# Fetching compression pages over two queues: two pages of each group of four by GpSimd, two by SyncE

## The reference

```python
old = pool[page_table].reshape(B, -1, N_KV_HEADS, HEAD_DIM)
...
def compress(rows, pe, w1, b1, w2):
    B, L, KV, DH = rows.shape
    n_chunk = L // STRIDE_CMP
    c = rows[:, :n_chunk * STRIDE_CMP].reshape(B, n_chunk, STRIDE_CMP, KV, DH)
    w1r = w1.reshape(BLOCK_CMP, DH, CMP_HID)
    lead = jnp.einsum('bnlkd,ldf->bnkf', c + pe[:STRIDE_CMP, None, :], w1r[:STRIDE_CMP])
    trail = jnp.einsum('bnlkd,ldf->bnkf', c + pe[STRIDE_CMP:, None, :], w1r[STRIDE_CMP:])
    hid = jax.nn.gelu(lead[:, :-1] + trail[:, 1:] + b1)
    return jnp.einsum('bnkf,fd->bnkd', hid, w2)
```

## Time and profile before

| | us |
|---|---|
| median of 3 runs | 3631.62 (3630.43 to 3634.85) |
| the profiled execution | 3631.43 |
| its span, first to last instruction | 3629.3 |
| PE busy in the span | 3364.7 (93%) |
| DVE busy | 1507.0 (42%) |
| ACT busy | 350.4 (10%) |
| POOL busy | 35.0 (1%) |
| mean granted TensorE clock | 0.961 |

### The profile page before, as it was taken

How to read it: one execution, slowest core, us unless ns; L and a number is a source line. 1 busy time by engine, 2 the same in 40 slices (tenths; PEclk the granted TensorE clock), 3 DMA queues, 4 the chain that set the end, 5 groups by cost and what they waited for, 6 DMA issues and landing times.

```text
span 3629.3 us, 41377 instructions
## 1 busy us (share of the span) xinstructions
PE 3364.7 (93%) x14936; PEld 2691.7 (74%) x14936; DVE 1507.0 (42%) x3114; ACT 350.4 (10%) x836; POOL 35.0 (1%) x70
## 2 busy tenths in 40 slices
PE   6999999799677789998879999999999999999996
PEld 4888878578445468857768888888888888888884
DVE  2698011244342110031154554455455545455554
ACT  2000021111331110011110000000000000000002
POOL 0000000100000000000000000000000000000000
PEclk8999999799888899999799999999999999999998
DMA  5222222333002442235222232223213212313221
GB/s 170 70 70 70 62 81 71 111 94 113 1 1 90 123 148 72 78 110 177 87 70 81 64 98 81 79 72 105 78 61 104 81 64 79 100 57 105 81 60 63
DMA packets 326040, 306.82 MB, mean 85 GB/s; under 512 B 12664, under 2 KB 312316, under 8 KB 324143
## 3 DMA queue, kind: packets, MB, share of 16 engines
q1 hardware_dynamic: 318490, 283.01, 25.0%
q0 software_dynamic: 3408, 18.69, 1.5%
q10 hardware_dynamic: 4032, 3.67, 0.3%
HBM read 291.36 MB, written 23.14 MB: 87 GB/s over the span
## 4 chain that ended last, share of the span: by engine, by line
PE 88%; DVE 4%; SPq 3%; ACT 3%; DMA 2%; issue 1%; POOL 0%; DVEq 0%; ACTq 0%; POOLq 0%
PE ps L1315 46%; PE ps L808 24%; PE ps L1011 5%; PE ps L803 3%; PE ps L832 2%; PE ps L1192 2%; ACT xT_region_b L1546 1%; PE ps L1050 1%; PE ps L1159 1%; SPq L712 1%; SPq L713 1%; PE ps L1280 1%; DVE xT_region_b L1717 1%; PE ps L1038 0%; PE ps L882 0%
## 5 line engine op out<-in xcount | busy, mean ns | idle before, releaser
L808 PE MATMUL ps<-xT_region_b,weight_ring 128*128 128x272 f32 x2560 | 588.1, 392 | 1.9 <-DVE region_c L1699 1.1
L808 PEld LDWEIGHTS ps<-xT_region_b,weight_ring 128*128 128x128 f32 x2560 | 486.1, 190 | 102.6 <-ACT v_tok L1450 1.3
L1315 PE MATMUL ps<-xT_region_b,weight_ring 128*128 128x272 f32 x2112 | 500.3, 393 | 11.1 <-DVE xT_region_b L2118 11.1
L1315 PEld LDWEIGHTS ps<-xT_region_b,weight_ring 128*128 128x128 f32 x2112 | 402.2, 191 | 94.7 <-issue 11.6
L1315 PE MATMUL ps<-region_f 128*128 128x272 f32 x1408 | 338.6, 394 | 5.5 <-DVE region_f L2145 5.5
L1315 PE MATMUL ps<-region_c,weight_ring 128*128 128x272 f32 x1408 | 339.5, 392 | 0.0
L1315 PEld LDWEIGHTS ps<-region_f 128*128 128x128 f32 x1408 | 268.4, 191 | 61.5 <-DVE region_f L2145 6.0
L1315 PEld LDWEIGHTS ps<-region_c,weight_ring 128*128 128x128 f32 x1408 | 267.4, 190 | 55.5 <-issue 0.5
L808 PE MATMUL ps<-region_f,weight_ring 128*128 128x272 f32 x1024 | 237.4, 395 | 10.4 <-DVE region_f L1717 10.4
L808 PEld LDWEIGHTS ps<-region_f,weight_ring 128*128 128x128 f32 x1024 | 196.1, 192 | 51.6 <-issue 10.8
L1764 DVE SCALAR_TENSOR_TENSOR rstd<-ext,tile_taps,rstd 128x512 f32<-128x512 f32 x240 | 180.5, 752 | 8.5
(11 more groups left out here) (286 smaller groups left out, 3268.3 us busy)
## 6 DMA issues: line engine op xcount, KB each, us to landing
weight_ring<-in_w_ffn_gate SPq DMA_DIRECT2D x44, 1024.0 KB, 4.9
weight_ring<-in_w_ffn_up SPq DMA_DIRECT2D x44, 1024.0 KB, 4.9
weight_ring<-in_w_in SPq DMA_DIRECT2D x36, 1024.0 KB, 5.2
weight_ring<-in_w_ffn_down SPq DMA_DIRECT2D x64, 512.0 KB, 4.0
weight_ring<-in_w_out SPq DMA_DIRECT2D x16, 1024.0 KB, 5.6
weight_ring<-in_w_ffn_down SPq DMA_DIRECT2D x32, 384.0 KB, 3.7
region_f<-in_cache_k_cmp SPq DMA_DIRECT2D x64, 128.0 KB, 2.0
region_f<-in_cache_v_cmp SPq DMA_DIRECT2D x64, 128.0 KB, 2.0
```

What stands on the lines that cost most here:

```text
L808: mm = pe.matmul(PS[:, 2 * j + h, 0:HALF], lhs(kt), rhs(kt, h), start=(kt == 0), stop=(kt == n - 1))
L1315: mm = pe.matmul(prod(k, r), lhs[:, t, :], rhs[:, t, :], start=(t == 0), stop=(t == m - 1))
```

## The change

Of each group of four pages, pages 0 and 1 are still fetched by SyncE, and pages 2 and 3 by GpSimd. GpSimd's fetches signal semaphores of their own, one for each buffer, and TensorE waits for both. In GpSimd's stream the 64 fetches stand behind the stores of the key and value rows and ahead of the wait for the memory's keys. Both queues wait alike for the buffer to be free. The W1 slabs stay with SyncE.

```diff
@@ -424,6 +424,7 @@
         s_w2 = sem("w2_loaded")
+        s_pgp = [sem(f"pages_loaded_by_pool{k}") for k in range(2)]
         s_fir = sem("cmp_operands_ready")
@@ -682,7 +683,7 @@
                 kind, half = divmod(p_, 2)
                 if step >= 2:
                     sp.wait_ge(s_tr, PAGE_AT[step - 2] + 2)
-                for k in range(4):
+                for k in range(2):
                     at = (half * 4 + b) * PAGES + pg4 * 4 + k
                     page = sp.value_load(PTB[0:1, at:at + 1], min_val=0, max_val=79)
                     sp.dma_start(PGS[step % 2][:, k, :],
@@ -954,7 +955,8 @@
             def page_turn(step):
-                pe.wait_ge(s_pg[step % 2], 64 * (step // 2 + 1))
+                pe.wait_ge(s_pg[step % 2], 32 * (step // 2 + 1))
+                pe.wait_ge(s_pgp[step % 2], 32 * (step // 2 + 1))
                 for kv in range(KV):
                     k = PAGE_AT[step] + kv
                     tr_bank(k)
@@ -2297,6 +2299,18 @@
                     else:
                         for b in range(NB):
                             store(O[12 + t][0, b, WIN - NT:WIN], rows[b * NT:(b + 1) * NT], s_kst[kk % 3])
+            pool.wait_ge(s_ptb, 16)
+            for step in range(32):
+                p_, r = divmod(step, 8)
+                b, pg4 = divmod(r, 2)
+                kind, half = divmod(p_, 2)
+                if step >= 2:
+                    pool.wait_ge(s_tr, PAGE_AT[step - 2] + 2)
+                for k in range(2, 4):
+                    at = (half * 4 + b) * PAGES + pg4 * 4 + k
+                    page = pool.value_load(PTB[0:1, at:at + 1], min_val=0, max_val=79)
+                    pool.dma_start(PGS[step % 2][:, k, :],
+                                   A[f"cache_{'kv'[kind]}_cmp"][0][ds(page, 1)].rearrange("o t k d -> (o t) (k d)")).then_inc(s_pgp[step % 2], 16)
             for k, dst in enumerate((KMT, VMT)):
                 pool.wait_ge(s_mke, k + 1)
                 store(O[10 + k][0, 0].rearrange("(a p) h d -> p a (h d)", p=P), dst, s_mst)
```

## The result

The changed kernel takes 3643.69 us (median of ten runs, 3638.11 to 3646.27), the kernel before 3631.8 us (ten runs, 3626.28 to 3637.58). The ratio is 1.0030, 95% interval 1.0021 to 1.0039: 8 to 14 us slower. The forecast was 3635.3 us with a range to 3645.0. The time lies in the range, but the likeliest case was a loss too small to be told from none, and a clear loss had 24%.

The account below looks back on a forecast made before the run. TensorE, busy 93% of the span, was taken as the bound, with SP's page issue bounding the page stage. +4.3 (page start and rounds) - 0.7 (group 20) + 0.3 (waits) = +3.9 us on 3631.43: 3635.3 us, range 3629.5 to 3645.

Parts of the forecast that it names:

- The late start: Page stage: group 0's turn must wait for GpSimd's row stores, starting at 679.0 instead of 665.42, 13.6 us late.
- the round: Groups 0 to 7, step from one pair of groups to the next: 1.97 + 0.77 + c + L = 6.2 us.
- rival 1: Groups 0 to 7: GpSimd's page costs 1.7 us or more, or arrives after 3.2 or more; 3643.6 us at 2.0; chance 23%.
- c: Price of one page on GpSimd: 1.27 us taken, range 0.50 to 2.0 us.
- L: Arrival, from GpSimd's last issue to TensorE's start on the page: 2.2 us taken, bounds 1.7 to 3.9.
- The two-port rule: Page stage: DVE's two-port copies stop GpSimd's DMA descriptors; estimate some +31 us, left out of the sum.
- The groups 8 to 31: Later page groups: GpSimd needs 5.5 us of the 13.3 us available, so its fetches stay hidden.
- Group 20: Value-cache wait of 6.44 us behind W1's slabs: only 0.7 us won, bounds 0 to 1.4 us.
- The clock: TensorE's granted clock, 1.2 GHz between page turns, was let come back to 2.4 GHz 4.3 us later too.
- rival 2: Denser page turns bring TensorE's clock back before the first product; first twelve products 3 us shorter, total 3628.5 us; chance 8%.
- The second wait on TensorE: One more wait on TensorE at each of 32 groups: 0.3 us taken, 0 to 1.6 us.
- the low end: Groups 0 to 7 with c = 0.5 and L = 1.7: last turn ends at 699.2, 1.4 us later.

## Why the prediction was right or wrong

**The late start held.** Forecast 13.6 us; the first turn stands 19.6 us after the row job instead of 6.2: 13.4.

**The price of a page held, the round did not.** A page costs GpSimd 1.15 us (forecast 1.27), which excludes the dear page of rival 1 (1.7 us or more); its late arrival, 3.2 us or more in all four places, did not come either, but with 2.5 to 3.2 us it was near. But the round was put at 1.97 + 0.77 + c + L = 6.2 us and took 7.4, 7.0 and 7.5. Two terms were too small: turn to GpSimd's first fetch, 1.2 us where I had SyncE's 0.77, and arrival, in the rounds 2.7 to 3.2 us where I had 2.2. Both had been read from neighbours, SyncE's wake-up and GpSimd's stores to HBM. My bound for L (up to 3.9) held them; the value taken did not. With 1.2, 1.15 and 3.0 the formula gives 7.3, the mean of the three. Group 7 was ready 6.7 us later, not 4.3.

**The two-port rule** changed nothing, as the row had suggested: GpSimd's 64 fetches took 546 ns in the median and none over 570, so no DVE copy lengthened one. "SBUF — State Buffer" of the Trainium skill, section "SBUF: two separate sides", wants a DVE copy in its two-port mode for that; the trace agrees where the one store at 664.5 us took 0.81 us.

**The groups 8 to 31** were hidden at their place, as forecast.

**Group 20** was put at -0.7 us and gave +0.1. I had written that "GpSimd's two pages come long before" the slabs. They did not, for GpSimd waits for the same turn as SyncE:

```profile
787.27 1.02 SPq L678 DMA_DIRECT2D weight_ring<-in_cmp_v_w  x2
```

```profile
787.47 0.55 POOL L2312 DMA_DIRECT2D region_f<-in_cache_v_cmp  x1 [0.60 <-issue]
```

The first of them, issued at 786.32, landed after 2.2 us; the second went out beside the slabs and took 4.9 us. The slabs landed later than before (5.9 and 8.3 us against 5.3 and 7.5), and the last of SyncE's two pages arrived 5.9 us after its fetch.

**The clock.** In the profile after, it came back before the end of the first products, 1.5 us of the 3.0 that rival 2 gives them, and none on the turns. That is no support for rival 2. In the kernel with the split in groups 0 to 7 alone, whose turns are as dense, the products took 6.04 us; in the kernel that fetches only groups 20 and 21 over GpSimd, whose first turns are those of before, they took 4.68; and one kernel shows both 4.61 and 6.04.

**The second wait on TensorE**, taken at 0.3 us, is not seen: from the first product to group 20's turn, over twelve split groups, the kernel with groups 8 to 31 split takes 92.9 us and the kernel before 93.0.

**What was missing** is the term of the end. I had written that GpSimd "has nothing else queued until 1605 us", and looked for its cost only where TensorE could wait for it. That term, put at nothing, measured 4.5 us. That the page stage's 4.4 us stand so near the forecast's 3.9 is luck: the start was 2.4 us later than forecast, the 0.7 us of group 20 did not come, and 2.4 us of clock that no term had held made up for most of it. It is luck too that the time lies in the range, whose upper end stood for a dear page and not for the end of the program. The row of the DRAIN (5.38 us behind 65 DMAs) was in the trace before; no other kernel stood beside it, so its dependence could not be read, but a cost between nothing and one more of its kind would have been a fair bound: 64 DMAs more, 5.3 us more. The experiment with 48 stores of 512 bytes shows the term by itself.

**Slips in the sums.** Sixteen fetches in a row have fifteen gaps: the end is 677.5 + 15c + L, at c = 2.0 709.7 and not 710.5. In the low end group 0 starts at 677.8, not 677.5. And the groups 8 to 31 stay hidden until c is 3.3, where two pages fill the 6.65 us of a group, not until 4. None of this moves the forecast.

The point of the change, four pages issued at 1.10 us by one queue, was right: the kernel with the fetches moved ahead of the stores is 6.6 us quicker in the stage. The change lost it by the place in GpSimd's order and by the number of its DMAs.

## What to carry to other kernels

When work is given to a second queue, first look at what stands in that queue at the moment when the first piece is needed, and let the old queue keep those pieces. Load addresses ahead of a wait, so that nothing but the fetch follows it. Issue a small fetch that is needed soon ahead of a large transfer, not behind it. And count the DMAs given to GpSimd: the end of the program belongs to the kernel's time, and the span behind the last store should be read in every profile.

## What the runs showed of the hardware

GpSimd's closing DRAIN costs 0.082 us for every DMA that GpSimd issued, from 65 to 113 DMAs, the same for page reads of 128 KB at 670 to 860 us and for stores of 512 bytes at 1640 us: (9.31 - 5.38) / 48. It levels out at 9.9 to 10.5 us from 129 to 161, and is 0.65 us at 193 in three executions of two kernels. What shortens it between 161 and 193 was not tried further.

A page number's load on GpSimd takes 0.286 us (SyncE 0.27), and its fetch of a page 0.546 us (SyncE 0.333); with the address arithmetic between them a page costs 1.15 against 1.10 us; the page lands after 2.6 us in the median, SyncE's after 2.0 in the kernel before.

A page of 128 KB that is fetched just behind two transfers of 1 MB is late from either queue: 4.6 to 5.8 us on GpSimd's (three pages of group 21 in the kernel that fetches groups 20 and 21 there), 5.3 us on SyncE's (the page issued at 787.03 before).
